# Sparse attention: compressed scores folded into the selected scores, eight steps between scores and transposes, ten row buffers

## The reference, cut to what matters

```
q, kc, vc, ks, vs, kw, vw, gate, z = split(u @ w_in)      # 16 heads of 64 in 4 groups
k_cmp, v_cmp = compress(kc), compress(vc)                 # 31 compressed keys and values a group
p_c = softmax(q . k_cmp + bias)      # compressed branch, 31 columns, causal by block
p_s = softmax(q . k_g   + bias)      # selected branch: top 8 blocks of 64 (all 8 at this length)
p_w = softmax(q . k_win + bias)      # window of 512 (the whole sequence here)
o = (gate0*p_c@v_cmp + gate1*p_s@v_g + gate2*p_w@v_win) * silu(z)
return o @ w_out
```

## Time and profile before

| | |
|---|---|
| Time, median of 3 runs | 2044.93 us (2043.79 to 2048.67) |
| Profiled execution, its own time | 2046.88 us |
| Span of the profiled execution | 2045.6 us |
| Granted TensorE clock, mean | 0.993 of full |
| Busy: TensorE / VectorE / ScalarE / GpSimd | 2014.7 / 1116.5 / 818.5 / 297.9 us |
| HBM | 90 GB/s over the span |

### The profile page before, as it was taken

How to read it: one execution, slowest core, us unless ns; L and a number is a source line. 1 busy time by engine, 2 the same in 40 slices (tenths; PEclk the granted TensorE clock), 3 DMA queues, 4 the chain that set the end, 5 groups by cost and what they waited for, 6 DMA issues and landing times.

```text
span 2045.6 us, 26834 instructions
## 1 busy us (share of the span) xinstructions
PE 2014.7 (98%) x10045; PEld 1635.7 (80%) x10045; DVE 1116.5 (55%) x2227; ACT 818.5 (40%) x1610; POOL 297.9 (15%) x426
## 2 busy tenths in 40 slices
PE   8999999999999999999999999999998999999998
PEld 6887888888888886788888888888887888877776
DVE  5438435666684335435535666694436663635456
ACT  5226333333342222333323333343338884335453
POOL 1103100000001120000010000031004663212311
PEclk8999999999999999999999999999998999999999
DMA  5330142332334331132242332235321103423212
GB/s 172 105 102 12 62 132 88 104 103 78 98 113 135 94 102 42 52 97 99 62 137 90 108 106 77 91 114 161 124 96 39 33 22 104 122 77 104 73 42 83
DMA packets 96915, 186.82 MB, mean 91 GB/s; under 512 B 8424, under 2 KB 16656, under 8 KB 96658
## 3 DMA queue, kind: packets, MB, share of 16 engines
q1 hardware_dynamic: 90162, 163.31, 25.3%
q0 software_dynamic: 6352, 21.27, 3.3%
q10 hardware_dynamic: 272, 0.52, 0.1%
HBM read 180.81 MB, written 4.26 MB: 90 GB/s over the span
## 4 chain that ended last, share of the span: by engine, by line
PE 91%; ACT 5%; DVE 3%; issue 1%; DMA 0%; POOL 0%; SPq 0%; ACTq 0%; DVEq 0%; POOLq 0%
PE bank L819 54%; PE bank L875 9%; PE bank L912 8%; PE bank L1427 5%; PE bank L1188 2%; PE bank L1348 1%; PE bank L1325 1%; PE bank L1441 1%; PE bank L963 1%; ACT sc L2012 1%; PE bank L1173 1%; PE bank L993 1%; PE bank L1464 1%; ACT xn L2006 1%; PE bank L1082 1%
## 5 line engine op out<-in xcount | busy, mean ns | idle before, releaser
L2188 DVE TENSOR_TENSOR wl<-raw,wh 128x1024 fp32r<-128x1024 f32 x320 | 395.8, 1241 | 652.4 <-ACT wh L1548 651.5
L1548 ACT ACTIVATE wh<-raw 128x1024 fp32r<-128x1024 f32 x320 | 336.9, 1057 | 716.0 <-PE bank L819 593.4
L819 PE MATMUL bank<-hTh,wh 128*128 128x512 f32 x1184 | 461.1, 389 | 0.2 <-issue 0.2
L819 PE MATMUL bank<-hTl,wh 128*128 128x512 f32 x1184 | 460.8, 389 | 0.0
L819 PE MATMUL bank<-hTh,wl 128*128 128x512 f32 x1184 | 460.8, 389 | 0.0
L819 PEld LDWEIGHTS bank<-hTh,wh 128*128 128x128 f32 x1184 | 222.3, 188 | 46.6 <-issue 0.3
L819 PEld LDWEIGHTS bank<-hTh,wl 128*128 128x128 f32 x1184 | 222.3, 188 | 46.2
L819 PEld LDWEIGHTS bank<-hTl,wh 128*128 128x128 f32 x1184 | 222.3, 188 | 45.9
L819 PE MATMUL bank<-wh,hTh 128*128 128x512 f32 x400 | 156.6, 391 | 0.1
L819 PE MATMUL bank<-wh,hTl 128*128 128x512 f32 x400 | 155.7, 389 | 0.0
L819 PE MATMUL bank<-wl,hTh 128*128 128x512 f32 x400 | 155.7, 389 | 0.0
(11 more groups left out here) (427 smaller groups left out, 3462.6 us busy)
## 6 DMA issues: line engine op xcount, KB each, us to landing
raw<-in_ffn_w_in SPq DMA_DIRECT2D x88, 512.0 KB, 3.5
raw<-in_ret_w_in SPq DMA_DIRECT2D x48, 512.0 KB, 3.7
raw<-in_ffn_w_out SPq DMA_DIRECT2D x44, 512.0 KB, 3.7
raw<-in_diff_w_in SPq DMA_DIRECT2D x32, 512.0 KB, 3.6
raw<-in_fox_w_in SPq DMA_DIRECT2D x23, 512.0 KB, 3.6
raw<-in_nsa_w_in SPq DMA_DIRECT2D x20, 512.0 KB, 3.5
raw<-in_ret_w_out SPq DMA_DIRECT2D x16, 512.0 KB, 3.6
raw<-in_fox_w_out SPq DMA_DIRECT2D x8, 512.0 KB, 3.5
```

The lines of the kernel that those rows point to most:

```text
L819: i = pe.do.matmul(dst, x, y, start=first and k == 0 and q == 0, stop=stop)
L1548: act.do.activation(M.hl[n % HL_SLOTS][0][:, 0:src.shape[1]], src, ACT.Copy).then_inc(*T.up("act_hi", n))
L2188: dve.do.tensor_tensor(wl[:, 0:m], src, wh[:, 0:m].bitcast(F32), ALU.subtract).then_inc(*T.up("dve_lo", n))
```

## The change

Five things change together.

1. Scores and transposes are eight steps apart instead of six (`AHEAD`), the products with the values twelve instead of ten, and there are ten row buffers (`ROWS`). Two of them are the two halves of one `raw` weight buffer; the load into that buffer (`LENT`, the last piece of `nsao`) waits for the transposes of tile 119.
2. The compressed keys of a group lie ahead of its selected keys in one tile (`a.cs`, `a.csl`: 32 + 512 columns). For the selected branch with i up to 2 (`beside(n)`) the two score matmuls take 32 columns more and give both kinds of scores. For i = 3 that doesn't fit a bank: `last_cmp_scores` does four matmuls of 32 columns per pair.
3. The compressed scores of both heads of a pair go into one tile `sc` [128, 8, 32]. VectorE takes the eight maxima one by one behind the tile's own, then subtracts them in one operation; ScalarE does one exponential of 256 columns without sum; VectorE sums and inverts; GpSimd weighs once; two transposes and one copy.
4. `take_q` writes the operands straight from PSUM: two activations and two VectorE operations of 64 partitions a tile, no scratch.
5. The last weight split ahead of the attention moves to step 16 on both engines, and ScalarE does one exponential ahead of the queries, which brings the load of its function table there.

```diff
+LENT = [load[0] for load in LOADS].index("nsao") + 7
+ROWS, AHEAD = 10, 8
...
+            a.cs, a.csl = sb(stack, "kcs", [128, 4, 32 + S], F32R), sb(stack, "kcsl", [128, 4, 32 + S], F32R)
+            a.rows += [M.raw[LENT % RAW_SLOTS][:, k * S:k * S + S] for k in range(2)]
+def beside(n):
+    return n % 16 < 6
...
     def load_weights(n):
+        if n == LENT:
+            sp.wait_ge(*at("pe_pt", ("nsa", 119)))
...  (GpSimd)
-        if n % 8 == 4:
-            pool.do.tensor_tensor(y[:, :, 2], y[:, :, 2], a.gate[:, :, 3 * h], ALU.mult)
-            pool.do.tensor_tensor(x[:, :, 0:31], x[:, :, 0:31], y[:, :, 2:3].to_broadcast([128, 4, 31]), ALU.mult)
+        if n % 16 == 11:
+            pool.wait_ge(*at("dve_cmp", (t, "recip")))
+            for par in range(2):
+                pool.do.tensor_tensor(y, y, a.gate[:, :, 3 * (2 * t + par)], ALU.mult)
+            pool.do.tensor_tensor(a.cp[:, :, :], a.cp[:, :, :], a.scs[:, :, 2:3].to_broadcast([128, 8, 32]), ALU.mult)
...  (TensorE)
-    def cmp_scores(h):
-        for i in range(4):
-            pe.do.matmul(M.bank[3][:, qs], query(M, h)[:, qs], a.kcmp[:, :, :], start=True, stop=False)
-            t = pe.do.matmul(M.bank[3][:, qs], query(M, h)[:, qs], a.kcml[:, :, :], start=False, stop=True)
+    def last_cmp_scores(t):
+        for par in range(2):
+            pe.do.matmul(out, query(M, h)[:, qs], a.cs[:, h // 4, 0:32], start=True, stop=False)
+            pe.do.matmul(out, query(M, h)[:, qs], a.csl[:, h // 4, 0:32], start=False, stop=True)
     def scores(n):
+        if beside(n):
+            x, y = a.cs[:, g, 0:32 + L], a.csl[:, g, 0:32 + L]
+            pe.free[b].append(("dve_cmp", (h, i, "max")))
+        else:
+            x, y = a.k[br][:, g, 0:L], a.kl[br][:, g, 0:L]
     def turn(n):
-        if n % 8 == 1:
+        if n % 16 == 7:
+            for par in range(2):
+                t = pe.do.transpose(M.bank[3][:, par * 128:par * 128 + 128], a.cp[:, 4 * par:4 * par + 4, :]...)
-        for n in (p - 6, p - 5):
+        for n in (p - AHEAD, p - AHEAD + 1):
             if 0 <= n < 128:
                 turn(n)
-        if p >= 10 and p % 4 == 2:
-            for n in (p - 10, p - 8):
+        if p >= AHEAD + 4 and p % 4 == 0:
+            for n in (p - AHEAD - 4, p - AHEAD - 2):
                 after(n)
-        if p % 8 == 0 and p < 128:
-            cmp_scores(p // 8)
+        if p % 16 == 2 and p < 128:
+            last_cmp_scores(p // 16)
...  (ScalarE)
-            act.do.activation(hi.bitcast(F32R), M.bank[...][:, :], ACT.Copy, scale=0.125)
             for par in range(2):
-                act.do.activation(query(M, 2 * t + par)[r:r + 64, :], hi[64 * par:64 * par + 64, :], ACT.Copy)
+                act.do.activation(query(M, 2 * t + par)[own, :], M.bank[...][own, :], ACT.Copy, scale=0.125)
+    act.do.activation(M.smalls[:, 1, 3:4], M.smalls[:, 0, 3:4], ACT.Exp).then_inc(*up("act_ahead", "table"))
     act_product(act, T, M, 4, 4, take_q(0))
-    act_product(act, T, M, 4, 4, take_q(4))
+    act_product(act, T, M, 3)
+    for o in range(4):
+        take_q(4)(o)
     def exp(n):
-        if n % 8 == 2:
-            for i in range(4):
-                act.do.activation(x, x, ACT.Exp, bias=y[:, 0:1], scale=-1.0, accum_out=y[:, 1:2])
+        if n % 16 == 8:
+            act.do.activation(a.cp[:, :, :], a.cp[:, :, :], ACT.Exp, scale=-1.0)
...  (ScalarE and VectorE, in their loops over n)
-        if 0 <= n - 6 < 128:
-            turned_out(n - 6)
+        if 0 <= n - AHEAD < 128:
+            turned_out(n - AHEAD)
+        if n == 16:
+            act_split(act, T, M)        # dve_split on VectorE
...  (VectorE)
-            dve.do.scalar_tensor_tensor(out=lo, in0=M.bank[...][:, :], scalar=0.125, in1=hi, op0=ALU.mult, op1=ALU.subtract)
             for par in range(2):
-                dve.do.tensor_copy(query(M, 2 * t + par)[64 - r:128 - r, :], lo[64 * par:64 * par + 64, :])
+                dve.do.scalar_tensor_tensor(out=q[other, :], in0=M.bank[...][own, :], scalar=0.125,
+                                            in1=q[own, :].bitcast(F32), op0=ALU.mult, op1=ALU.subtract)
     def largest(n):
-        if n % 8 == 2:
-            for i in range(4):
-                dve.do.tensor_tensor_reduce(a.sc[h % 2][:, i, 0:k], M.bank[3][:, c:c + k], bias, ...)
-        if n % 8 == 4:
-            dve.do.reciprocal(y[:, :, 2], y[:, :, 1])
+        if br == 0:
+            dve.do.tensor_tensor_reduce(a.sc[:, m, 0:k], src[:, c:c + k], bias, ...)
+        if n % 16 == 7:
+            dve.do.tensor_tensor(a.cp[:, :, :], a.sc[:, :, :], a.scs[:, :, 0:1].to_broadcast([128, 8, 32]), ALU.subtract)
+        if n % 16 == 10:
+            dve.wait_ge(*at("act_cmp", t))
+            dve.do.reduce_sum(a.scs[:, :, 1], a.cp[:, :, :], AX.X)
+            dve.do.reciprocal(a.scs[:, :, 2], a.scs[:, :, 1])
```

More of the change, by code:

```diff
@@ L684, in pool_nsa @@
         load_bt(h)
+    pool.wait_ge(*at("pe_cmp", "values"))
+    for w in range(2):
+        pool.wait_ge(*at("act_hid", w))
+    pool.do.memset(a.sc[:, :, :], BIG).then_inc(*up("pool_blank", "scores"))
     def weigh(n):
         h, br, i = nsa_tile(n)
-        buf, cell = a.rows[n % 8][:, 0:128 * (i + 1)], M.smalls[:, n % CELLS, 2:3]
+        buf, cell = a.rows[n % ROWS][:, 0:128 * (i + 1)], M.smalls[:, n % CELLS, 2:3]
         pool.wait_ge(*at("dve_gate", "any"))
@@ L713, in after @@
             pool.do.tensor_tensor(ol, a.prod[:, :], oh.bitcast(F32), ALU.subtract).then_inc(*up("pool_o", t))
-    for n in range(128 + 10):
+    for n in range(128 + AHEAD + 4):
         if n < 128:
@@ L719, in pool_nsa @@
             weigh(n - 1)
-        if 0 <= n - 10 < 128:
-            after(n - 10)
+        if 0 <= n - AHEAD - 4 < 128:
+            after(n - AHEAD - 4)
     T.note("pool", "nsa attention")
@@ L1362, in after @@
             pe.free[b] = [("dve_o", t)]
-    for p in range(0, 128 + 10, 2):
+    for p in range(0, 128 + AHEAD + 4, 2):
         for n in (p, p + 1):
@@ new lines, in largest @@
+        if n % 16 == 7:
+            t = n // 16
+            for par in range(2):
+                dve.wait_ge(*at("dve_cmp", (2 * t + par, 3, "max")))
+            if t:
+                dve.wait_ge(*at("pe_cmp", ("turned", t - 1)))
+            dve.do.tensor_tensor(a.cp[:, :, :], a.sc[:, :, :], a.scs[:, :, 0:1].to_broadcast([128, 8, 32]), ALU.subtract).then_inc(
+                *up("dve_cmp", (t, "below")))
+        if n % 16 == 10:
+            t = n // 16
+            dve.wait_ge(*at("act_cmp", t))
+            dve.do.reduce_sum(a.scs[:, :, 1], a.cp[:, :, :], AX.X).then_inc(*up("dve_cmp", (t, "sum")))
+            dve.wait_ge(*at("dve_cmp", (t, "sum")))
+            dve.do.reciprocal(a.scs[:, :, 2], a.scs[:, :, 1]).then_inc(*up("dve_cmp", (t, "recip")))
```

170 lines of the change are left out of this document (76 added, 94 removed).

## The result

| | before | after |
|---|---|---|
| Time, median of 14 runs each | 2043.97 us (2043.46 to 2048.67) | 2049.42 us (2047.48 to 2050.49) |
| Profiled execution, its own time | 2046.88 us | 2047.55 us |
| Span of the profiled execution | 2045.6 us | 2046.3 us |
| Busy: TensorE / VectorE / ScalarE / GpSimd | 2014.7 / 1116.5 / 818.5 / 297.9 us | 2007.4 / 1118.6 / 797.0 / 298.3 us |

The ratio is 1.002, 95% interval [1.0013, 1.0027]: no change by the bound of 0.3%, though the interval lies wholly on the slow side, and the two medians are 5.45 us apart. The forecast was 2045.6 us, with a range to 2053. ScalarE has 21.5 us less to do and TensorE 7.3, and nothing of it arrives at the end.

What follows compares the result with a forecast made beforehand. TensorE, with 91% of the path, was taken to bound the kernel. Beginning -4.2, six pairs +3.1 and end +1.8 gave +0.7 us: profiled 2047.6, less 1.95 for the median, 2045.6 us, range 2033 to 2053.

Steps and rivals of the forecast that it cites:

- The mechanism: In each pair, transposes behind the i = 3 and i = 1 scores wait for banks to be emptied, together 2.4 us.
- TensorE's work: Matmul work of a pair of heads, without the old waits: 16.99 us, after fewer compressed-score matmuls.
- The pair: Each of six even pairs takes 19.3 us for 18.77, +3.1 us over the six.
- The beginning: Start of the attention up to iteration 18: 4.2 us earlier, or 7.3 were the clock to stay up.
- and behind them two VectorE operations: Last query tile before the attention: two VectorE operations of 0.69 us after two activations, done at 1542.95.
- so I take it as half until 1560: Clock at the attention's start taken as half until 1560: nine us of work at half rate.
- The end: From iteration 114 to the output product: 25.2 us for 23.40, +1.8, with twelve steps of uncovered transposes and products.
- The step from the profile to the median: Whole kernel: the median taken as 1.95 us below the profiled execution, so 2047.6 becomes 2045.6 us.
- A: Pairs: the wait for ScalarE's small exponentials is traded for waits behind the 512-column scores; 2045.6 us, chance 0.55.
- B: Pairs: new waits don't come because lighter ScalarE runs ahead; a pair takes 17.0 us, the whole 2031; chance 0.25.
- C: Pairs: waits come larger as subtraction, sum or split cost more; priced at 1.1 us more a pair, 2053; chance 0.14.
- D: Pairs: the clock falls again there, costing up to 8.5 us, 2054; chance 0.06.

Runs made afterwards that it cites:

- six_split_end: The changed kernel with the old distance of six steps and the weight split moved behind the last copy of the transposes: 2040.23 us, ratio 0.9978.
- six_cover: six_split_end with the value products of i = 3 one iteration later, ahead of the transposes, and compressed transposes two steps later: 2041.02 us, ratio 0.9982.
- products_spread: The changed kernel with the value products of two tiles in every iteration, ahead of its transposes, instead of four in every second: 2035.73 us, ratio 0.9958.
- late_subtract: The changed kernel with VectorE's subtraction of the compressed maxima moved behind its copy out of bank 5: 2047.38 us, ratio 1.0009.
- six_filler: six_split_end plus eight unused matmuls of 128 columns where the kernel before had its compressed scores: 2042.72 us, ratio 0.9992.
- six_steps: The changed kernel with the old distance of six steps, value products ten steps behind: 2046.43 us, ratio 1.0008.
- entry_alone: The kernel before with only the direct queries, the early table load and the split behind step 16: 2046.72 us, ratio 1.0004.
- after_split_end: The changed kernel with only the weight split moved behind the last copy of the transposes: 2047.43 us, ratio 1.0014.

## Why the prediction was right, and where it wasn't

**The mechanism held.** The waits came where they were put and for the reason given. I take each one as the time from where the next matmul could follow the last scores (0.11 us behind their start, 0.18 with 384 columns) to the value products, less what the transposes between take without a wait (0.31 us for two in six_split_end, 0.80 for six in six_cover). In the rows above, 1607.38 - 1605.80 - 0.31 = 1.27. Predicted and measured: behind i = 3, window branch, 0.5 and 0.60; selected branch 1.1 and 1.27; behind i = 1, window 0.7 and 0.83; selected 0.1 and 0.12. Sum 2.4 and 2.82.

**TensorE's work held.** 19.73 - 2.82 = 16.91 us, for 16.99. The narrow matmuls that no row showed have the pace of the 128-column ones (0.11 us apart), as taken. products_spread supports it: 17.82 with hardly a wait and twice the changes.

**The pair was mis-sized by 0.43 us**, in the waits, and not in the chains. The copies that empty bank 5 end as added up:

```profile
1606.40 0.67 DVE L2970 COPY pTn<-bank 128x512 f32<-128x512 f32 x1
1612.40 0.36 ACT L2032 ACTIVATE pTn<-bank 128x256 f32<-128x256 f32 x1
1616.54 0.69 DVE L2970 COPY pTn<-bank 128x512 f32<-128x512 f32 x1
```

Counted from the start of their scores (1603.49, 1609.93 and 1614.10) they end at 3.58, 2.83 and 3.13 us, for 3.5 to 3.6, 2.75 and 3.1. What the sum lacked are the ends: 0.05 to 0.06 us from a copy to the weight load behind it, 0.26 from a single transpose to the products, and in the selected branch TensorE is there at 2.31 for 2.4. These made 2.82 of the 2.4, and the 0.1 by which I let one wait shorten the next did not appear. late_subtract shows the largest single part to be as costed (0.42 for the subtraction, 0.45 measured). Six pairs came to +5.8 instead of +3.1, once the split's 1.4 us are put where I had counted them.

**The beginning was mis-sized by as much, on the other side.** First maximum and exponential came within 0.06 us of the forecast, which is luck: the first scores were 0.82 us early in this execution, and from them to the first maximum it took 3.03 us for the 2.27 added up. The step that failed there is "and behind them two VectorE operations": VectorE has all four tiles' eight in a row, from 1537.03 to 1542.76, 0.71 us each and hardly a gap. Tile 18 came at 1558.53, or 1559.9 with the split's 1.4 us, for 1563.7: the step that failed is "so I take it as half until 1560". The clock was at half for 3.4 us, and -9.34 + 1.4 = -7.9, or -7.1 from the first scores on, is close to the -7.3 that the prediction gave for a clock that stays up. **The end** gave 2.7 for 1.8: two waits for ScalarE's copies (0.57 and 0.26 us) that I had left out.

**The sum** of the three errors is -3.7 + 2.7 + 0.9 = -0.1, so the profiled execution was forecast at 2047.6 and took 2047.55. That is luck in the sizes, not in the mechanism.

**The step from the profile to the median failed by 3.8 us.** I took from the profiled time the 1.95 us by which the kernel before lay above its median. The new kernel's profiled execution is the second fastest of 14 and lies 1.87 below its median. So the traces, 0.7 us apart, hide most of the 5.45 us between the medians: 2.91 us because the traced execution of the kernel before is slow for its kernel (2046.88 for a median of 2043.97), 1.87 because the traced one of the kernel after is fast for its own.

For the first part the record has a likely reason. The traced execution of the kernel before has a mean clock of 0.993, with 17 us at half in the beginning of the attention. In the 90 executions beside the experiments, the 33 with a mean clock of 0.998 took 2043.3 to 2044.1 us and the 10 with 0.992 took 2048.1 to 2048.9. A mean of 0.998 over 2045 us is about 4 us of missing clock (half of the time at half clock), up to 5 with the rounding, and the traced execution misses 8.5 in the beginning of the attention alone. So most executions can't have had that stretch in full, and there was less in them for the change to save. Those executions weren't traced, so where their clock was low isn't shown. The second part isn't the clock: at a mean clock of 0.997, that of the traced execution, the kernel after took 2047.48 to 2050.49 us. Its cause stays open.

**The rivals.** A, traded waits, was right. B's assumption, that ScalarE's lighter load would shorten the pair, was wrong at both distances; six_filler shows that it rested on counting removed matmuls as gain. My own reading after the result made the same mistake: in six_steps I expected the 17.0 us of bare work. C had the right places, with 0.4 us more a pair than forecast, not 1.1; the median, 2049.42, lies half way between A's 2045.6 and C's 2053. D, the clock falling in the pairs, did not occur in the changed kernel (clock 1.00 over the 119.87 us), but its mechanism is real: after 2.66 us without a matmul it fell in six_steps, after 2.12 us at the split of entry_alone, and after 1.44 us at the split of products_spread; after the 1.35 us at the split of the changed kernel it did not. The Trainium skill ("TensorE: Matmul & The Clock Gate", HAM oscillation — how this bites in real kernels) says of a kernel whose matmuls stop for a transfer between bursts that each gap puts the clock down; the traces of six_steps, entry_alone and products_spread agree for their one long gap, and the changed kernel's pairs, with four waits each, don't.

**Where the gain went.** TensorE's 1.28 us less a pair are paid out only if TensorE has something else to do while scores go through VectorE and ScalarE and back to a free bank. The old order had that something in the very matmuls removed. The distance of eight, which alone is a loss of 5.2 us a pair, pays only when the value products stand in front of the waiting transposes; whether six steps would do as well in that order was not run.

## What to carry to other kernels

Before counting removed work as gain, ask which wait it covered: a group of matmuls between two dependent steps is free up to the length of the chain beside it. When one engine's order is written by hand, follow for each buffer the chain from its producer to its release, and put independent work exactly in front of the instruction that waits for it; the same matmuls in a better place were worth 13.7 us here, and sixteen unused ones put back in each pair cost 0.2 of their 1.86 us. A job shared by two engines in sequence, as the split, stalls a third that waits for both; its 2.3 us cost a pair 1.4, 3.6 and 5.6 us here (after, entry_alone, six_steps), the larger two with half clock behind the stall. Put it where nobody waits. And before a forecast is built on one trace, compare its time and mean clock with those of the other executions: here the stretch that promised most was longer in the traced execution than it can have been in the median one.

## What the runs showed of the hardware

The granted clock in one stretch isn't a property of the kernel alone. The changed kernel and after_split_end have the same beginning of the attention up to step 16, and the 4 us from 1548 show 0.90 in the trace of one and 0.63 in that of the other. At the start of the program, where these kernels do the same, the clock is low until about 18 us in the trace of the kernel before and 16 in that of the kernel after, and it doesn't fall there at all in those of six_split_end, six_filler and six_cover; of the 4 us from 8 us on TensorE was busy 1.83 in the kernel before and 3.90 in six_split_end. The 4 us from 1916, behind the changed part, show 0.58 in late_subtract and 1.00 in the kernel after, though TensorE was idle for the same 1.45 of 24 us around it in both. And a single idle time of 2.66 us in the midst of dense work was followed by some 7 us at half clock, so that the stall cost more than twice itself.
